# RWKV preparation with merged scans and a short reciprocal, rotary tables moved, and norm outputs in banks by c and c + 4

## What is computed

```python
def token_shift_mix(p, mu):
    prev = jnp.pad(p, ((0, 0), (1, 0), (0, 0)))[:, :-1]
    return p + mu * (prev - p)
...
    log_w = -DECAY_SCALE * jax.nn.sigmoid((w0 + jnp.tanh(w_lo) @ w_up).astype(jnp.float32))
    w = jnp.exp(log_w)
    a = jax.nn.sigmoid(a0 + a_lo @ a_up)
...
    kk = hd(k * k_k).astype(jnp.float32)
    kk = kk * lax.rsqrt(jnp.maximum(jnp.sum(kk * kk, axis=-1, keepdims=True), 1e-24))
    k = k * (1.0 + (a - 1.0) * k_a)
...
def rms_norm(x, g):
    xf = x.astype(jnp.float32)
    y = xf * lax.rsqrt(jnp.mean(xf * xf, axis=-1, keepdims=True) + RMS_EPS)
    return (y * g.astype(jnp.float32)).astype(x.dtype)
```

## Time and profile before

| | |
|---|---|
| median of 3 runs (lowest, highest) | 1797.06 us (1794.25, 1800.37) |
| profiled execution, its own time | 1792.22 us |
| its span, first to last instruction | 1790.4 us |
| TensorE matmul busy | 1661.9 us (93%) |
| VectorE, ScalarE, GpSimd busy | 1015.1, 839.6, 70.8 us |
| mean granted TensorE clock | 0.954 |
| chain that ended last | PE 85%, DVE 9%, ACT 3% |
| weights | 244 loads of 1 MB, 147 GB/s over the span |

### The profile page before, as it was taken

One profiled execution on the slowest core, in us unless ns is written; L12 is line 12 of the kernel. 1 busy time (PEld: TensorE's weight loads), 2 busy tenths in 40 slices (PEclk: granted clock), 3 DMA queues, 4 the chain that ended last, 5 costly groups with the idle time before them and its releaser, 6 DMA issues.

```text
span 1790.4 us, 29315 instructions
## 1 busy us (share of the span) xinstructions
PE 1661.9 (93%) x11992; PEld 1513.4 (85%) x11992; DVE 1015.1 (57%) x1344; ACT 839.6 (47%) x1267; POOL 70.8 (4%) x76
## 2 busy tenths in 40 slices
PE   7679868989999899999689999999999999999999
PEld 6678758879999899987469999899989977789998
DVE  4874565455455655464855455645568834565554
ACT  5434135454444544455345444544457653554443
POOL 1210000000000000000300000000000004200000
PEclk9899979999999899999799999999999995799999
DMA  6230024424555354544314554455544450045553
GB/s 240 85 128 2 2 71 153 165 106 165 188 186 179 140 189 180 184 172 157 116 71 165 188 186 179 167 179 189 183 163 164 167 187 24 26 174 181 189 186 115
DMA packets 37080, 263.63 MB, mean 147 GB/s; under 512 B 4224, under 2 KB 4352, under 8 KB 5760
## 3 DMA queue, kind: packets, MB, share of 16 engines
q1 hardware_dynamic: 35712, 257.97, 40.0%
q0 software_dynamic: 704, 2.62, 0.4%
q10 hardware_dynamic: 576, 1.79, 0.3%
HBM read 261.31 MB, written 1.05 MB: 147 GB/s over the span
## 4 chain that ended last, share of the span: by engine, by line
PE 85%; DVE 9%; ACT 3%; issue 1%; DMA 1%; POOL 0%; POOLq 0%; SPq 0%; DVEq 0%; ACTq 0%
PE PS L387 25%; PE PS L388 25%; PE PS L389 25%; PE PS L596 2%; PE PS L619 2%; PE PS L917 1%; DVE w_lo L1398 1%; PE PS L381 1%; PE PS L492 1%; DMA raw_weights<-W 1%; DVE h_lo L1422 1%; PE PS L516 1%; DVE arena L1652 1%; PE PS L896 1%; PE PS L895 1%
## 5 line engine op out<-in xcount | busy, mean ns | idle before, releaser
L1398 DVE TENSOR_TENSOR w_lo<-raw_weights,w_hi 128x1024 fp32r<-128x1024 f32 x488 | 598.8, 1235 | 554.9 <-ACT w_hi L966 554.6
L966 ACT ACTIVATE w_hi<-raw_weights 128x1024 fp32r<-128x1024 f32 x488 | 514.4, 1058 | 554.9 <-PE PS L389 540.1
L387 PE MATMUL PS<-h_hi,w_hi 128*128 128x256 f32 x2320 | 664.7, 286 | 31.5 <-DVE h_lo L1422 16.2
L388 PE MATMUL PS<-h_lo,w_hi 128*128 128x256 f32 x2320 | 661.1, 285 | 0.0
L389 PE MATMUL PS<-h_hi,w_lo 128*128 128x256 f32 x2320 | 660.7, 285 | 0.0
L387 PEld LDWEIGHTS PS<-h_hi,w_hi 128*128 128x128 f32 x2320 | 450.0, 194 | 37.7 <-DVE w_lo L1398 16.1
L388 PEld LDWEIGHTS PS<-h_lo,w_hi 128*128 128x128 f32 x2320 | 450.3, 194 | 2.2 <-issue 0.5
L389 PEld LDWEIGHTS PS<-h_hi,w_lo 128*128 128x128 f32 x2320 | 449.9, 194 | 0.0
L387 PE MATMUL PS<-w_hi,g_hi 128*128 128x512 f32 x440 | 171.8, 390 | 0.0
L388 PE MATMUL PS<-w_lo,g_hi 128*128 128x512 f32 x440 | 171.8, 390 | 0.0
L389 PE MATMUL PS<-w_hi,g_lo 128*128 128x512 f32 x440 | 171.2, 389 | 0.0
(11 more groups left out here) (338 smaller groups left out, 1319.9 us busy)
## 6 DMA issues: line engine op xcount, KB each, us to landing
raw_weights<-W SPq DMA_DIRECT2D x244, 1024.0 KB, 4.8
post_gain<-post_gains POOLq DMA_DIRECT2D x3, 512.0 KB, 4.1
x_resid<-x SPq DMA_DIRECT2D x2, 512.0 KB, 6.8
arena<-mem POOLq DMA_DIRECT2D x1, 1024.0 KB, 5.2
out<-x_resid SPq DMA_DIRECT2D x2, 512.0 KB, 2.6
ptab<-cols ACTq DMA_DIRECT2D x1, 857.0 KB, 8.8
ctab<-consts ACTq DMA_DIRECT2D x1, 710.0 KB, 5.7
rtab<-rows ACTq DMA_DIRECT2D x1, 176.0 KB, 11.3
```

Of the source, the lines that this page charges most:

```text
L387: mm(out, lhs[0], rhs[0], start=start, stop=False)
L388: mm(out, lhs[0], rhs[1], start=False, stop=False)
L966: A(w_hi[:, n % H, :], raw[:, n % (2 * R), :], ACT.Copy).then_inc(S.hi_ready, 1)
L1398: v.tensor_tensor(w_lo[:, n % H, :], raw[:, n % (2 * R), :], w_hi[:, n % H, :].bitcast(F32), ALU.subtract).then_inc(S.lo_ready, 1)
```

## The change

- **Mixes.** ScalarE writes (1 - mu) p from PSUM straight to `Q`, two activations for a slot, and VectorE adds mu times the shifted PSUM tile in place. `pin`, its zero columns and GpSimd's subtractions go. TensorE may write a bank again when the mix is done (`q_mixed`), not when it is copied.
- **`k` scaling.** 1 + (a - 1) k_a is one activation for each of four tiles on ScalarE (Identity with scale and bias); VectorE does one product.
- **Scans.** One scan over 16 blocks of 65 columns for the product and one for its inverse; a zero column in the decay and a one in the second operand restart each block. GpSimd writes these columns ahead.
- **`kk` normalisation.** The sums go to 32 rows for each tile in one bank (`pair32`), maximum, root and reciprocal run over 256 columns, and four matmuls with `spread` bring the factors back to banks 4 to 7. The product with `kk` reads PSUM and stands behind the last mix. TensorE waits for the reciprocal behind slot 6, and for `kk_used` behind slot 8, ahead of the bonus sum.
- **Copies behind the transposes.** ScalarE makes all six; VectorE's bonus product signals `bonus_ready`, for which the transposes of `kk` wait.
- **Rotary tables.** VectorE's angles and ScalarE's sine stand behind the second block of the first FFN.
- **Norms.** Tiles c and c + 4 share a bank; the transposes go 0, 4, 1, 5, ...; `h_lo[c]` waits for `h_hi[c]` alone, `h_hi[c]` from 4 on waits for `h_lo[c - 4]`, and the first half waits for each low part; `ms` is computed ahead of the first rows' scaling; ScalarE's third split stands behind the high parts. The first slot behind a norm writes a bank that the transposes don't use (FFN gate and up 0 and 1, `xbc` 2).

The diff, cut to its core:

```diff
+        c65 = lambda ap: ap.rearrange("p (s t) -> p s t", s=16)
+        Pc_r, dec65 = pin_r[:, 2558:3598], pin_r[:, 1024:2064]
+        inv65 = arena[:, invP_at:invP_at + 1040]
+        ones65 = xn_t[:, 0:1040]
+        inv16 = c65(inv65)[:, :, 1:65]
...
+        def xbc_bank(n):
+
+            return 4 + n % 4 if n else 2
+
+        def gate_bank(b):
+
+            return 4 + 2 * (b % 2) if b else 0
...
-                    for n in range(7):
-                        if n == 3:
-                            pool.wait_ge(S.kkraw_ready, 1)
-                            tt(tmp, kk, kk, ALU.mult).then_inc(S.kksq_ready, 1)
-                        pool.wait_ge(S.pin_ready, 1 + n)
-                        if n:
-                            pool.wait_ge(S.q_mixed, n)
-                        tt(tshift.rearrange("p (c t) -> p c t", c=2), pin[:, n % 4, :, 0:T], pin[:, n % 4, :, 1:T + 1],
-                            ALU.subtract).then_inc(S.diff_ready, 1)
+                    pool.wait_ge(S.xT_ready, 4)
+                    nc.gpsimd.memset(ones65, 0.0).then_inc(S.zero_ready, 1)
+                    pool.wait_ge(S.zero_ready, 1)
+                    nc.gpsimd.memset(c65(ones65)[:, :, 0:1], 1.0)
+                    nc.gpsimd.memset(c65(dec65)[:, :, 0:1], 0.0)
+                    nc.gpsimd.memset(c65(inv65)[:, :, 0:1], 0.0).then_inc(S.zero_ready, 1)
+                    pool.wait_ge(S.kkraw_ready, 1)
+                    tt(tmp, kk, kk, ALU.mult).then_inc(S.kksq_ready, 1)
...
-                    for c in range(KC):
-                        if t == 0 and c == 0:
+                    for i, c in enumerate((0, 4, 1, 5, 2, 6, 3, 7)):
+                        if t == 0 and i == 0:
                             pe.wait_ge(S.xn_ready, 3 * k + 1)
-                        if t and c in (0, 2):
-                            pe.wait_ge(S.xn_ready, 3 * k + 2 + c // 2)
-                        at = c % 2 * 256 + t * P
-                        last = nc.tensor.transpose(PS[:, 4 + c // 2, at:at + P], src[:, t, c * P:(c + 1) * P], ident)
-                        if t and c % 2:
+                        if t and i in (0, 2):
+                            pe.wait_ge(S.xn_ready, 3 * k + 2 + i // 2)
+                        at = c // 4 * 256 + t * P
+                        last = nc.tensor.transpose(PS[:, 4 + c % 4, at:at + P], src[:, t, c * P:(c + 1) * P], ident)
+                        if t and i % 2:
...
-                    if normed is not None and c % 2 == 0:
-                        pe.wait_ge(S.hT_ready, 8 * normed + c + 2)
+                    if normed is not None:
+                        pe.wait_ge(S.hT_ready, 8 * normed + c + 1)
...
-                    pe.wait_ge(S.pin_ready, n - 3)
+                    pe.wait_ge(S.q_mixed, n - 3)
...
-                    for c in range(2):
-                        last = mm(PS[:, 4 + c, :], cn("pair"), tmp[:, c * 512:(c + 1) * 512], start=True, stop=True)
+                    for c in range(4):
+                        last = mm(PS[32 * c:32 * c + 32, 4, 0:T], cn("pair32"), tmp[:, c * T:(c + 1) * T], start=True,
+                                  stop=True)
                     last.then_inc(S.kksum_done, 1)
+                if n == 6:
+
+                    pe.wait_ge(S.kkmax_step, 3)
+                    pe.wait_ge(S.g_ready, 1)
+                    for c in range(4):
+                        rows_ = slice(32 * c, 32 * c + 32)
+                        last = mm(PS[:, 4 + c, 0:T], cn("spread")[rows_, :], tmp[rows_, 0:T], start=True, stop=True)
+                    last.then_inc(S.kkmax_step, 1)
                 if n == 8:
 
                     pe.wait_ge(S.bonus_in, 1)
+                    pe.wait_ge(S.kk_used, 1)
...
-                    act.wait_ge(S.xT_ready, 4 * k + c // 2 + 1)
-                    A(h_hi[:, c, :], PS[:, 4 + c // 2, c % 2 * T:(c % 2 + 1) * T], ACT.Copy, scale=pc("gain", 8 * k + c))\
+                    act.wait_ge(S.xT_ready, 4 * k + c % 4 + 1)
+                    if c >= 4:
+                        act.wait_ge(S.hT_ready, 8 * k + c - 3)
+                    A(h_hi[:, c, :], PS[:, 4 + c % 4, c // 4 * T:(c // 4 + 1) * T], ACT.Copy, scale=pc("gain", 8 * k + c))\
                         .then_inc(S.hT_hi, 1)
 
             def norm(k, after=None):
                 stats(k, X, k - 1)
+                to_h(k)
...
+                if f == 0:
+                    act.wait_ge(S.trig_step, 1)
+                    A(trig, trig, ACT.Sin).then_inc(S.trig_step, 1)
...
-                    if n >= 4:
-                        act.wait_ge(S.q_mixed, n - 3)
-                    A(pin[:, n % 4, :, 1:T + 1], PS[:, n % 4, :].rearrange("p (c t) -> p c t", c=2), ACT.Copy)\
-                        .then_inc(S.pin_ready, 1)
+                    for j in range(2):
+                        c = [12, 4, 6, 0, 2, 8, 10][n] + j
+                        last = A(Q[:, c, :], PS[:, n % 4, j * T:(j + 1) * T], ACT.Copy, scale=mu_rest[:, c:c + 1])
+                    last.then_inc(S.pin_ready, 1)
...
-                    A(invP, decay, ACT.Exp, scale=DECAY).then_inc(S.decay_ready, 1)
-                    act.wait_ge(S.decay_ready, 1)
-                    A(decay, decay, ACT.Exp, scale=-DECAY).then_inc(S.decay_ready, 1)
+                    for c in range(4):
+                        last = A(tmpb[:, c * T:(c + 1) * T], a_f[:, c * T:(c + 1) * T], ACT.Identity,
+                                 bias=ka_rest[:, c:c + 1], scale=pc("k_a", c))
+                    last.then_inc(S.ka_ready, 1)
+                    A(inv16, decay.rearrange("p (s t) -> p s t", s=16), ACT.Exp, scale=DECAY)
+                    A(c65(dec65)[:, :, 1:65], decay.rearrange("p (s t) -> p s t", s=16), ACT.Exp, scale=-DECAY)                        .then_inc(S.decay_ready, 1)
...
-                    A(tmp, tmp, ACT.Sqrt).then_inc(S.kkmax_step, 1)
+                    A(tmp[:, 0:T], tmp[:, 0:T], ACT.Sqrt).then_inc(S.kkmax_step, 1)
...
-                v.tensor_scalar(dst[:, 0, :], src[:, 0, :], rstd[:, 0:1], None, ALU.mult).then_inc(S.xn_ready, 1)
                 dve.wait_ge(S.ssq_ready, k + 1)
                 v.tensor_scalar(ms[:, 1:2], ssq[:, 1:2], 1.0 / D, 1e-6, ALU.mult, ALU.add).then_inc(S.ms_ready, 1)
+                v.tensor_scalar(dst[:, 0, :], src[:, 0, :], rstd[:, 0:1], None, ALU.mult).then_inc(S.xn_ready, 1)
                 dve.wait_ge(S.std_ready, 2 * k + 2)
                 step(v.reciprocal(rstd[:, 1:2], std[:, 1:2]))
-                for hs in (slice(0, 256), slice(256, 1024)):
-                    v.tensor_scalar(dst[:, 1, hs], src[:, 1, hs], rstd[:, 1:2], None, ALU.mult).then_inc(S.xn_ready, 1)
+                two = lambda ap: ap[:, 1, :].rearrange("p (a b) -> p a b", a=2)
+                for hs in (slice(0, P), slice(P, 512)):
+                    v.tensor_scalar(two(dst)[:, :, hs], two(src)[:, :, hs], rstd[:, 1:2], None, ALU.mult)\
+                        .then_inc(S.xn_ready, 1)
...
-                    dve.wait_ge(S.hT_hi, 8 * k + c // 2 * 2 + 2)
-                    v.scalar_tensor_tensor(h_lo[:, c, :], PS[:, 4 + c // 2, c % 2 * T:(c % 2 + 1) * T],
+                    dve.wait_ge(S.hT_hi, 8 * k + c + 1)
+                    v.scalar_tensor_tensor(h_lo[:, c, :], PS[:, 4 + c % 4, c // 4 * T:(c // 4 + 1) * T],
...
+            def angles():
+
+                dve.wait_ge(S.pos_loaded, 16)
...
-                    last = v.scalar_tensor_tensor(Q[:, c + j, :], tshift[:, j * T:(j + 1) * T], pc("mu", c + j),
-                                                  pin[:, n % 4, j, 1:T + 1], ALU.mult, ALU.add)
+                    last = v.scalar_tensor_tensor(Q[:, c + j, 1:T], PS[:, n % 4, j * T:(j + 1) * T - 1], pc("mu", c + j),
+                                                  Q[:, c + j, 1:T], ALU.mult, ALU.add)
...
-            dve.wait_ge(S.a_ready, 1)
-            for c in range(4):
-                last = v.tensor_scalar(tmpb[:, c * T:(c + 1) * T], a_f[:, c * T:(c + 1) * T], -1.0, pc("k_a", c),
-                                       ALU.add, ALU.mult)
-            step(last)
-            step(v.scalar_tensor_tensor(k_f, tmpb, 1.0, k_f, ALU.add, ALU.mult))
+            dve.wait_ge(S.ka_ready, 1)
+            step(v.tensor_tensor(k_f, tmpb, k_f, ALU.mult))
...
-            dve.wait_ge(S.decay_ready, 2)
-            for q in range(16):
-                last = v.tensor_tensor_scan(Pc[:, q, 1:65], decay[:, q * 64:(q + 1) * 64], cn("zeros"), 1.0,
-                                            ALU.mult, ALU.add)
-            last.then_inc(S.scan_done, 1)
-            for q in range(16):
-                qs = slice(q * 64, (q + 1) * 64)
-                last = v.tensor_tensor_scan(invP[:, qs], invP[:, qs], cn("zeros"), 1.0, ALU.mult, ALU.add)
-            step(last)
+            dve.wait_ge(S.decay_ready, 1)
+            dve.wait_ge(S.zero_ready, 2)
+            v.tensor_tensor_scan(Pc_r, dec65, ones65, 0.0, ALU.mult, ALU.add).then_inc(S.scan_done, 1)
```

(23 more changed lines are left out.)

82 lines of the change are left out of this document (40 added, 42 removed).

## The result

The changed kernel takes 1776.6 us (median of 4 runs, 1775.59 to 1777.11) against 1795.65 us for the kernel before, run beside it (1792.53 to 1800.37): a ratio of 0.9891, 95% interval 0.9867 to 0.9915. The forecast was 1785.0 us, range 1776 to 1791. The sign and the places were right, the gain too small: the median fell by 19 us for 12, and between the two profiled executions (that of the kernel before was one of its shorter ones) the span fell by 16.6 us, not 12.05.

What follows compares the result with a forecast made beforehand. TensorE, streaming weights, was taken as the bound, losing time only in holes and at low clock. Gains of 2.4 + 4.9 + 0.45 + 4.3 = 12.05 us took the median from 1797.06 to 1785.0 us, range 1776 to 1791.

Steps and rivals of the forecast that it cites:

- Start of the half behind the scans: First projection: the `w_lo` behind scans and Newton step comes 2.4 us sooner, TensorE starting at 70.8 instead of 73.2.
- the two stops: VectorE's waits for GpSimd's `r` and `k` products, at the first Newton operation (2.3 us) and next `w_lo` (2.35).
- From there to the end of the projection: TensorE from that half to 110: 5.7 (hole gone) + 3.35 - 2.45 (low clock) - 1.7 (spread matmuls) = 4.9 us.
- the clock's term: Projection: work at half clock loses TensorE 2.45 us, against 3.35 before; the fall comes 3.5 us into the hole.
- Hand-over: Projection to scores: six copies on ScalarE end at 116.65, where VectorE's last ended at 117.1; 0.45 us less.
- Norms: First products sooner at most norms behind the first: 4.3 us together, bounds 2 and 6.
- The post norms: The two norms behind post norms start at clock 0.50; gain 0.3 to 0.63 us, taken as 0.45 each.
- (1): Rival: GpSimd's products don't stop VectorE; hole under 1 us, no fallen clock, 7.1 us more, 1778; chance 0.22.
- (2): Rival: the norms give nothing, eaten by the half-speed stretch and the `ms` step; 1789; chance 0.10.
- (4): Rival: the rotary block in the first FFN is not covered; costs 2 us, 1787; chance 0.05.
- (5): Rival: ScalarE and VectorE wait for each other in `to_h`, losing 3.7 us a norm; about 1819; chance 0.04.
- (3): Rival: merged scans take 2.9 us each, plus a third hole or longer low clock; 1789 to 1790; chance 0.09.

Runs made afterwards that it cites:

- second profiles: Kernel before and changed kernel each run once more, unchanged: 1794.54 us and 1777.9 us.
- the preparation alone: Changed kernel with its norm part taken out (old norm boundary), run beside the kernel before: 1787.95 us, ratio 0.9957.

## Why the prediction was right, and where it was short

**Start of the half behind the scans: forecast 2.4, measured 3.1** (73.22 to 70.13). VectorE came 0.4 sooner than 58.3, the scans took 2.3 each for 2.0, and the two stops cost 1.81 and 1.87 us (3.04 - 1.23, 4.22 - 2.35) for 2.3 and 2.35, since the products took 2.0 and 2.17 us and not 2.35. In the second profiles of both kernels the same start moved by 2.3 (72.77 to 70.45), so the 3.1 is not firm. The Trainium skill (DVE: opcode table, instruction layouts, handler registers and perf-mode slots; Datapath and trigger behaviour) has the scan at half throughput; the estimate of 2.2 us worked out from it was nearer to the 2.3 of the trace than my 2.0, though the sum with it would have been no nearer. By the Trainium skill (SBUF — State Buffer; Who interferes with whom) an instruction of VectorE with two SBUF inputs and one of GpSimd that reads SBUF contend for one read interface. The trace agrees, in both directions: GpSimd's product stood for the scan (4.06 us for 2.2), and VectorE's Newton operation for the product (3.04 for 1.23).

**From there to the end of the projection: forecast 4.9, measured 6.27.** The hole of 5.71 went, and in this execution the low clock cost about what was forecast (TensorE worked 4.17 us in it, so 2.09 lost, for 2.45). Mis-sized was the term of the spread matmuls: 0.71 us, not 1.7. I priced them by the 128-row `pair` multiplication (1.89 for 8 passes), but the four use 32 rows each, a different quarter of the array, and 8 passes took 0.71. With it, 5.71 + 3.35 - 2.09 - 0.71 = 6.26. The four `pair32` multiplications, forecast to cost what the wide ones did, took 0.64 for 1.89; they stand ahead of a hole, so that gave nothing. That the clock's term came out near is partly luck. The forecast had the clock fall 3.5 us into the hole again; it fell 1.9 and 5.2 us into it. In the second profiles the old kernel worked 12.06 us at the low clock and the new one 6.05, so this term was 3.0 us and not 1.26 (0.9 forecast), and the stretch gained 7.17 (38.53 to 31.36). The whole projection gained 9.36 and 9.49.

**Hand-over, rotary tables, the split behind the high parts**: 0.47, nothing and nothing, as forecast (0.45 for the first); the second and third are shown by undoing them.

**Norms: forecast 4.3, measured 7.97** for the stretches that hold them (0.82 + 3.54 + 1.06 + 1.62 + 0.93); alone on the kernel before they brought 8.5 us (6 to 14 by the interval of the ratio). At a plain norm 0.80 to 0.82 for 0.6: the term mis-sized is that of the `ms` operation, taken as a cost of up to 0.15 and worth a gain of 0.21; the rest of the norm gave 0.59 where 0.38 + 0.36 were forecast. Before `wq` 0.82 for 0.75, and before `q` 0.45 for 0.25; the other 0.6 us of that row lie inside the attention and are not explained. The post norms were the largest miss: 1.54 and 2.00 for 0.45 each. The second profiles and the preparation alone show that little of it is the work of the norm itself: the old code itself gave 197.78, 196.37 and 196.37 at the first and 197.88, 198.47 and 196.37 at the second, with 3.41 to 10.24 us of low clock. At equal lengths (6.83 at the first) the old code gives 196.37 and the new 196.24; at the second the new one gains 0.49 on the old one's shortest. The rest of the 3.5 us goes with how long the clock was low. All ten profiled executions with the new norm had 6.83 and 3.41 us there. At the second post norm all three of the old code had more (10.24, 10.24, 6.83), which speaks for the new code; at the first the old one had 10.24, 6.83 and 3.41. Why is not shown.

**The clock in the scores: forecast nothing, measured a loss of 2.77** up to 189, of which 1.53 came back by 219. It can't be put down to the change: the same stretch (from the `kk` transposes) took 78.63 and 80.02 in two executions of the kernel before, 81.40 and 80.67 in two of the kernel after, and 78.65 to 81.71 in the rest. The norms alone on the kernel before, where this stretch is the old code, took 81.40 too. The time goes with the low clock in the stretch: 78.63 to 80.45 us with 6.83 us of it, 80.02 and 80.67 with 10.24, 81.40 to 81.71 with more. What sets how often the clock falls there stays open.

**The rivals.** (1) fell as a description of this kernel, and was roughly right as a price: with GpSimd held back 5.2 us are to be had, where it had 7.1, since it let the hole fall under 1 us, and 2.26 stayed. (2), (4) and (5) fell to the norm alone, the rotary tables back, and the plain norms' 0.35. (3) had scans of 2.9 us and a new hole; they took 2.3, and no new hole came.

## What to carry to other kernels

Where VectorE feeds the engine that sets the time, look at what GpSimd does beside it: holding two GpSimd products back brought 5 us, and a new order on VectorE, with one product beside a one-input operation and two behind a lead of two weight halves, another 6, with no operation removed. A hole costs its length and the work done at the low clock behind it: with the products held back the half behind the hole started 3.4 us sooner (70.13 to 66.77), no low clock followed, and the projection ended 4.5 us sooner. What the low clock cost in the projection was 3.35 and 6.03 us (half of the work done in it) in two executions of the same kernel before, so take a second profile before that term is trusted. And price a small matmul by its own rows and columns, not by a full one in the same place.
